# Spacing of 1280 gathered row tiles in a one-core transformer step: by transfer time that each planned step leaves over

## What is computed

```python
h = rmsnorm(x, g0) * (1 + sc1) + sh1          # scale, shift, gate from silu(cond) @ w_mod
u, v, zb, q, k, rv, rg_f, rg_b, gm = split(h @ w_in)
y_a = gelu(u) * (mix128x128(layernorm(gelu(v))) + b)
y_b = pooled means of zb (windows 2, 4, 8, 16), times pool_w
y_c = bidirectional retention of q, k, rv, gated by silu(rg_f), silu(rg_b)
x = x + gt1 * ((ga * y_a + gb * y_b + gc * y_c) @ w_out)
h2 = rmsnorm(x, g1) * (1 + sc2) + sh2
# PEER: 8 heads, each top 16 of 128 + 128 keys, top 16 of their 256 sums
act = gelu(einsum('thkd,td->thk', u_tab[expert], h2))
x = x + gt2 * einsum('thk,thkd->td', softmax(best) * act, v_tab[expert])
y = rmsnorm(x, final_norm_g)
```

## The kernel before

| stage | steps | what | TensorE | VectorE | weight units | ranking steps | rows |
|---|---|---|---|---|---|---|---|
| 1 | 163-249 | retention heads, group 0 ranked | 201.2 | 147.2 | 3 | 36 | 74 |
| 2 | 250-297 | retention heads | 173.2 | 32.6 | 1 | 0 | 42 |
| 3 | 298-339 | pooling | 220.8 | 11.2 | 10 | 0 | 52 |
| 4 | 340-390 | group 1 | 244.0 | 58.5 | 16 | 0 | 62 |
| 5 | 391-412 | queries of group 1 | 63.6 | 48.0 | 4 | 15 | 26 |
| 6 | 413-432 | ranking | 13.2 | 54.4 | 0 | 17 | 22 |
| 7 | 433-470 | group 2: v, u, ga | 136.8 | 61.9 | 6 | 12 | 63 |
| 8 | 471-523 | group 2: the rest | 229.2 | 76.0 | 10 | 4 | 90 |
| 9 | 524-575 | queries of group 2 | 114.2 | 124.8 | 4 | 39 | 81 |
| 10 | 576-591 | ranking | 1.0 | 48.0 | 0 | 15 | 24 |
| 11 | 592-609 | group 3: v, u | 63.0 | 27.9 | 3 | 6 | 46 |
| 12 | 610-631 | group 3: u, ga, mix | 80.8 | 39.5 | 4 | 7 | 56 |
| 13 | 632-682 | group 3: the rest | 222.2 | 76.9 | 9 | 5 | 134 |
| 14 | 683-719 | queries of group 3 | 92.4 | 86.4 | 4 | 27 | 93 |
| 15 | 720-734 | ranking, last queries | 21.8 | 38.4 | 0 | 12 | 31 |
| 16 | 735-769 | ranking | 1.0 | 105.8 | 0 | 33 | 35 |
| tail | | rows alone | | | | | 349 |

## Time and profile before

### The profile page before, as it was taken

The page is one execution under the profiler, slowest core; times in us unless marked ns, Lnnn a source line. Parts: engine busy times, 40 slices in busy tenths (PEclk is TensorE's granted clock), DMA queues, the critical chain, the costliest instruction groups (busy, mean ns, idle before and its releaser), DMA issues. The chain is left out here.

```text
span 4783.5 us, 44034 instructions
## 1 busy us (share of the span) xinstructions
PE 3840.5 (80%) x11761; PEld 1567.2 (33%) x11761; DVE 2843.5 (59%) x6525; ACT 1638.0 (34%) x5132; POOL 1617.0 (34%) x1312
## 2 busy tenths in 40 slices
PE   6999799999998869999785897888776456676666
PEld 4645355564444323353331231342222001111110
DVE  1112587566576685754699656545688974544544
ACT  4110254332122343433344433333443443333333
POOL 0000023222222233333343434443333245455454
PEclk8999899999999879999896997999887556666666
DMA  7544688889899989999999999999999789999998
GB/s 260 214 184 185 219 310 311 290 310 355 340 399 394 357 311 398 395 382 382 371 380 343 400 377 384 406 396 407 409 399 382 291 319 421 407 421 415 414 421 351
DMA packets 290057, 1687.28 MB, mean 353 GB/s; under 512 B 29136, under 2 KB 71184, under 8 KB 111120
## 3 DMA queue, kind: packets, MB, share of 16 engines
q0 software_dynamic: 184320, 1342.26, 70.3%
q1 hardware_dynamic: 97472, 318.79, 17.6%
q10 hardware_dynamic: 8016, 23.42, 1.5%
HBM read 1646.57 MB, written 37.78 MB: 352 GB/s over the span
## 5 line engine op out<-in xcount | busy, mean ns | idle before, releaser
L993 POOL DMA_INDIRECT slots<-in_peer,idxR x1280 | 1610.8, 1258 | 3110.6 <-PE ps L1289 1924.3
L1289 PE MATMUL ps<-slots,lhs 128*64 128x512 f32 x4544 | 1523.3, 784 | 736.3 <-ACT lhs L1044 714.9
L1558 DVE CUSTOM_DVE_ANT_0 slots<-slots,h2R 128x1024 f32<-128x1024 f32 x1280 | 1547.6, 1224 | 792.8 <-issue 726.3
L1273 PE MATMUL ps<-ring,arena 128*128 128x512 f32 (+1 forms) x3996 | 1588.8, 555 | 52.1 <-DMA ring<-in_wq 19.0
L1273 PEld LDWEIGHTS ps<-ring,arena 128*128 128x128 f32 x3996 | 767.9, 196 | 894.8 <-issue 819.9
L1289 PEld LDWEIGHTS ps<-slots,lhs 128*64 128x64 f32 x4544 | 297.0, 160 | 1856.1 <-ACT lhs L1044 1596.7
L1033 ACT ACTIVATE gelus<-dots 128x1 f32<-128x1 f32 x1280 | 256.1, 200 | 1525.1 <-DVE dots L1558 1504.1
L1044 ACT ACTIVATE lhs<-fold,wgts 128x64 f32<-128x64 f32 x1136 | 395.0, 348 | 37.2
L1036 ACT ACTIVATE wgts<-gelus,gsmR 128x1 f32<-128x1 f32 x1280 | 377.1, 295 | 42.1
L1273 PE MATMUL ps<-ring,slots 128*128 128x512 f32 (+1 forms) x704 | 249.1, 515 | 0.0
L1570 DVE SCALAR_TENSOR_TENSOR slots<-slots,wgts 128x1024 f32<-128x1024 f32 x135 | 173.1, 1283 | 81.4 <-ACT wgts L1036 75.7
(11 more groups left out here) (197 smaller groups left out, 2344.7 us busy)
## 6 DMA issues: line engine op xcount, KB each, us to landing
ring<-in_whead SPq DMA_DIRECT2D x24, 2048.0 KB
ring<-in_wa SPq DMA_DIRECT2D x24, 2048.0 KB
ring<-in_wq SPq DMA_DIRECT2D x16, 2048.0 KB
slots<-in_peer,idxR POOLq DMA_INDIRECT x1280
ring<-in_wlate SPq DMA_DIRECT2D x16, 1024.0 KB
ring<-in_wgc SPq DMA_DIRECT2D x16, 1024.0 KB
ring<-in_wgb SPq DMA_DIRECT2D x8, 2048.0 KB
ring<-in_wout SPq DMA_DIRECT2D x8, 2048.0 KB
```

What stands on the lines that cost most here:

```text
L993: g.indirect_dma_start(out=slot(R), out_offset=None, in_=a["peer"], in_offset=bass.IndirectOffsetOnAxis(ap=idxR[:, p % KEEP, g2, col:col + ...
L1273: done = mm(out, lhsT, rhs, start=n == 0, stop=n == len(pairs) - 1)
L1289: done = mm(ps[j * HALF:(j + 1) * HALF, g2, :], weights, slot(R)[:, D + j * UW:D + (j + 1) * UW], start=start, stop=stop)
L1558: v.tensor_tensor_reduce(out=u, in0=u, in1=h2R[:, g2, :], scale=1.0, scalar=0.0, op0=ALU.mult, op1=ALU.add, accum_out=dots[:, R % LHS:R % ...
```

## The change: rows spaced by what the steps leave over

`wall` is replaced by `spare_time()`. It runs two clocks over the front, one with TensorE's planned costs and one with VectorE's, and lets neither lag the other by more than 20 us (`AHEAD`). A step's share is how far the later clock moves, less 5.3 us (`UNIT_TIME`) where the step opens a weight unit; it may be negative. The pace of the last span goes from one row in 2.9 us of wall time to one in 1.5 us of spare time. The planned VectorE cost of a ranking step goes from 3.0 to 3.2.

```diff
-LAST_PACE = 2.9
+ROW_TIME, UNIT_TIME, AHEAD = 1.5, 5.3, 20.0
...
-                          act=.8 * (hd == 0 and part == "c") + 2.4 * (hd == 1 and part == "b"), dve=3.0)
+                          act=.8 * (hd == 0 and part == "c") + 2.4 * (hd == 1 and part == "b"), dve=3.2)
...
-        wall = [max(ev.cost) for ev in self.front]
         starts = [self.ready[BASE[k], int(len(cs) > 2)] for k, cs in enumerate(GROUPS)] + [len(self.front)]
+        spare = self.spare_time()
...
-            total = sum(wall[a:b])
-            rows = min(len(cs) * ROWS, total / LAST_PACE if k == len(GROUPS) - 1 else len(cs) * ROWS)
+            total = sum(spare[a:b])
+            rows = min(len(cs) * ROWS, total / ROW_TIME if k == len(GROUPS) - 1 else len(cs) * ROWS)
...
-                spent += wall[n]
+                spent += spare[n]
...
+    def spare_time(self):
+
+        pe = dve = clock = 0.0
+        spare = []
+        for ev in self.front:
+            pe, dve = pe + ev.cost[0], dve + ev.cost[2]
+            pe, dve = max(pe, dve - AHEAD), max(dve, pe - AHEAD)
+            spare.append(max(pe, dve) - clock - UNIT_TIME * ev.first)
+            clock = max(pe, dve)
+        return spare
```

## The result

The changed kernel takes 4814.0 us (median of 6 executions, 4812.8 to 4823.8) and the kernel before, on the same chip, 4776.5: a ratio of 1.008, 95% interval 1.0068 to 1.0093. The forecast was 4708, range 4675 to 4768. The profiled execution has a span of 4812.3 us, against 4783.5.

The account below looks back on a forecast made before the run. The prediction took the transfer queues as the bound, full at 415 GB/s but dry in parts of stages 1 to 16. Tail -90 and front +25 made -65, from 4773 to 4708 us, range 4675 to 4768.

Parts of the forecast that it names:

- What bounds the kernel: Whole kernel: transfer queues, dry for 415 of 3307 us over stages 1 to 16; a row moved there saves 2.56 us.
- the tail: Row tiles after the front: 349 rows become 314, at 2.56 us each, 90 us less.
- the placement: Rows per stage by the plan's costs: 966 ahead of the front's end, not 931; stage 16 alone gains 36.
- the sum over the front: Stages 1 to 16: gains and losses both 180 us; +25 taken for lumpier placement, ends -20 and +69.
- three needs: Each front stage lasts as long as the largest of its transfer, TensorE and VectorE needs; all 16 came within 24 us.
- charge for lumps: Front: eight slots hold 20 us of transfers, so shorter pieces were priced, -20 to +69 us; +25 taken.
- The full rate of 415: Transfer queues: 415 GB/s taken as their full rate, from the tail's 417.
- the chained rows: Stages 2 and 3: 16 more, 1.28 us of VectorE each, covered by TensorE's need; cost nothing, without cover 20 us.
- The slower one: Rival, chance 0.12: thinned stages don't get shorter; 4791 us with 60% of their gain lost, 4863 with all.
- the -180: Front: summed gain of the stages that get shorter, set against +180 us in the stages that get longer.
- The partial one: Rival, chance 0.12: the tail shrinks by 90 us but lumps cost 69; -21, 4752 us.
- GpSimd's wait for TensorE: From 3375 to 3880 us: 293.7 us of waiting for slots, read as waiting for rows to be placed.

Follow-up runs that it names:

- mix: Changed kernel with the first two spans spaced by wall time and the third by spare time without the unit's 5.3 us: 4725.5 us, 0.989.
- lumped: Kernel before, with stage 8's 90 rows lumped: none behind a step that opens a unit, up to four behind the others: 4800.9 us, 1.0055.
- before_lag4: Kernel before with TensorE four rows behind VectorE instead of three: 4749.0 us, 0.9941.
- cap3: Changed kernel with at most three rows behind any one step, the rest going to the next steps: 4777.8 us, 0.9996.
- lag4: Changed kernel with TensorE four rows behind VectorE instead of three: 4789.8 us, 1.0021.
- even: Changed kernel with the unit's 5.3 us spread over all the unit's steps, not taken from the first: 4755.0 us, 0.9951.
- even_lag4: Changed kernel with the unit's 5.3 us spread over the unit's steps and TensorE four rows behind VectorE instead of three: 4770.0 us, 0.9984.
- cap3_2: Changed kernel with at most three rows behind a step, and at most two in steps 250 to 390: 4786.6 us, 1.0011.
- ret_few: Changed kernel with at most three rows behind a step, and 8 rows instead of 27 beside stage 2's retention steps: 4786.5 us, 1.0015.
- last_only: Kernel before with only the last span's pace changed, 1.456 instead of 2.9: 4734.4 us, 0.9899.

## Why the prediction was wrong

**What bounds the kernel, the tail, the placement: right.** The tail's row cost 2.57 us and 35 rows left it: -89. Stage 16 took 195 us at 397 GB/s (forecast 194 and 395), stage 13 is full at 409 GB/s and took 475 (484), stage 11 took 83 (90). The counts of the stages are those of the table of the change (stage 16 shows 143 records of L1569, two a row). Fetches beside ranking cost nothing, as taken. By the rule of the Trainium skill (DMA: Bandwidth & Descriptors, "Where 436 GB/s comes from") that HBM binds a core at about 358 GB/s, the kernel's 1687 MB need 4713 us, an estimate. That leaves 60 us under 4773, not the "next to nothing" of the prediction, and no kernel here went below it (mix, the lowest, took 4725), so the totals don't decide. The rates do: the tail and stage 13 run at 416 and 409 GB/s, and the trace disagrees here too.

**The step that failed is the sum over the front, +25 where +118 was measured.** Each stage was given the largest of three needs, and TensorE's waits for the engines in front of it were put at nothing; the one charge for lumps, 25 us, was for something else. Two stretches show it, stage 8 and stages 2 to 4.

*The charge for lumps was worked out for the wrong thing.* The prediction saw that no row would stand beside a step that opens a unit and up to nine elsewhere, and priced that by how long eight slots of transfers last, in pieces of three or four steps. What decides is the distance between VectorE and TensorE: three rows are ready when a step ends, and a fourth has to pass through VectorE and ScalarE behind that step's own work. In stage 8 this cost 25 us more than before. Shown by lumped (18.5 us by lumps alone, 1 us with one more row of distance) and by the waits of six kernels:

| stage 8 | before | before_lag4 | after | cap3 | lag4 | lumped |
|---|---|---|---|---|---|---|
| rows | 90 | 90 | 105 | 105 | 105 | 90 |
| time, us | 322.7 | 310.9 | 376.3 | 351.1 | 348.8 | 341.2 |
| TensorE waits for lhs, us | 13.8 | 1.8 | 38.9 | 17.6 | 11.9 | 33.7 |

From each kernel to its neighbour of equal rows the time changes by the wait, to within 4 us. Sums of busy time can't show this, since the wait is TensorE's idle time between two steps while all three engines have room on average.

*The full rate of 415 is not what failed.* Stage 8 was forecast at TensorE's need of 335 us, with transfers at 334 just under it, and cap3, lag4 and even all stop at 346 to 351, at 398 to 403 GB/s. But even_lag4 does these 105 rows in 342 us at 410 GB/s, and before_lag4 does stage 13, which has nine weight units, at 414:

```profile
2919.00:3335.00 416.00, 364.65 (x1149) 149.26 (x1146) 237.53 (x424) 158.12 (x488) 162.49 (x135) 0.92 1.01 414
```

So at most 19 of stage 8's +54 us are a need of transfers or of TensorE, and the forecast had 14 of these. The other 35 went with spacing and distance, and the wait for `lhs` fell by 31, from 38.9 to 7.7.

*In stages 2 to 4 the chained rows do delay the front.* Forecast +3, measured +53 (28.0, 7.5 and 17.7). The prediction laid 16 more chained rows and the added dots under TensorE's need, because VectorE's total was lower. But VectorE works in program order. The waits of TensorE, 856 to 1560 us in the kernel before and 845 to 1602 in the changed one:

```profile
PE ps L1388 <- DVEq L1740: 14.9, 13, 1.8
...
PE ps L1289 <- DVE slots L1570: 7.6, 2, 4.9
...
PE ps L1479 <- DVE arena L1858: 5.5, 1, 5.5
```

```profile
PE ps L1399 <- DVEq L1751: 25.1, 12, 4.2
PE ps L1300 <- DVE slots L1581: 16.1, 5, 5.7
...
PE ps L1490 <- DVE arena L1869: 11.0, 1, 11.0
```

These three add 24 us, of 31 that TensorE idles more by the two tables: dense work of VectorE that TensorE needs comes later behind dots and chain additions. The other 22 us are busy time (660.8 against 638.9). Its products for rows are 8.6 of that, since most of the 19 rows more are chained. The remaining 13 go with the granted clock, which is 0.93, 0.96 and 0.92 in these stages and was 0.97, 0.97 and 0.96; the products of stage 2's retention, the same 64 in both kernels, are longer for it (before, then changed):

```profile
L1388 PE MATMUL ps<-arena,tmp 128*128 128x256 f32 x64 | 22.2, 431 | 21.7 <-DVEq L1740 14.9 <-DVEq L1722 6.7
```

```profile
L1399 PE MATMUL ps<-arena,tmp 128*128 128x256 f32 x64 | 24.8, 476 | 30.8 <-DVEq L1751 25.1 <-DVEq L1733 5.7
```

So 46 of the 53 have a name. That reading is from the traces of two kernels and no run isolates it, nor whether the clock fell because TensorE idled more; cap3_2 and ret_few, which tried the three stages, only took two other explanations away. even shows that spacing is part of it (262 in place of 279 us in stage 4, same rows). The last 7 us stay open.

**The rest.** Stages 6, 9 and 14, which rank, took 17, 16 and 20 us more than forecast. In all three, TensorE was under 80% busy in both kernels, the queues under 0.92 in the changed one, and VectorE at 97 of 113, 206 of 256, 172 of 232 us. Spacing bears on stage 6: even took 102 us for it in place of 113, with 30 rows and not 31. Of stages 9 and 14 no run shows the cause.

**The rivals.** The slower one ended on the right side (18 to 90 us slower; it was 38) by the wrong mechanism: thinned stages did get shorter (1, 5, 7, 11 and 12 within 3 us of the forecast or better, 9 and 14 by half and two thirds; stage 4 alone got 18 us longer), and its point of decision, half of the -180 lost, was not reached: the eight thinned stages gave -140. It was the thickened ones that paid 259 instead of 180. The partial one blamed lumps, rightly, but priced them by the slots and not by the distance, and its 69 us, from the finest cuts, was still 49 short. The chance of 0.12 for slower left out that +180 could be too low. And GpSimd's wait for TensorE, read as rows waiting to be placed, is there in the changed kernel too (3480 to 4000):

```profile
PEld ps L1300 <- ACT lhs L1055: 293.2, 134, 11.0
POOL slots L1004 <- PE ps L1300: 290.7, 111, 13.3
```

It didn't fall with rows placed by spare time, so it does not show what the prediction read in it. A slot also stays held while TensorE waits; that this is the reason is not shown.

**What the runs say of the change's parts.** That the price of the lumps is the wait at distance three is shown for stage 8; for the rest of the front it is argued. The dense last span is worth -45 us, spare time without the unit's term in the third span perhaps 9 more (mix against last_only, which their intervals don't tell apart), and the unit's charge on its first step costs 59 (even against the change).

## What to carry to other kernels

Where two streams are interleaved in program order at a fixed distance, the distance says how many items may stand between two steps of the other stream: count the longest lump against it before summing busy times, since item n + 1 pays the chain of the engines in front (up to 2.5 us here, 1.6 on average over the 25 waits of stage 8). A cost that is spread in time, such as the transfer of weights over three steps, is to be charged over those steps; charging it to the step that issues it makes lumps. And more distance is not free: it holds buffers, and one row of it, a gain of 0.6% in one placement, was a loss of 0.3% in another (even_lag4 against even).

## What the runs showed of the hardware

A queues' share of 1.00 does not mean that a stage can't move its bytes faster. Stage 13 of the kernel before read 1.00 at 403 GB/s; with TensorE one row further behind, the same stage moved them at 414 (share 1.01). Stage 8 with 105 rows read 1.00 at 403 GB/s in lag4 and 1.01 at 410 in even_lag4. The tail, where gathers go alone, moved 416 to 417 GB/s at 1.01. So stages that mix 2.1 MB weight units with gathers came within 1 to 2% of the tail's rate, and what is told from a share near 1 alone is uncertain by some 3%.

TensorE's granted clock fell in stages 2 and 4, where it idled more. In stage 2 its mean is 0.93 with 34 us idle and was 0.97 with 22, and a retention product of 431 ns took 476. Which of the two came first no run shows.
